# A stick-breaking and RWKV-7 block with 32 experts: weights in transfers of 512 KB, experts in an order that alternates the groups, scatters counted by buffer

## The reference

```python
group_logits = (hf @ w_rg)                       # 4 groups
group_idx = jnp.argmax(group_logits, axis=-1)
group_gate = take(softmax(group_logits), group_idx)
exp_logits = (hf @ w_re).reshape(n_tok, 4, 8)    # 8 experts a group
in_group = take(exp_logits, group_idx)
top_p, top_i = lax.top_k(softmax(in_group), 2)
gates = group_gate * top_p / sum(top_p)
eid = group_idx * 8 + top_i                      # two experts a token, one group
y[token] = sum over the two of gate * ((silu(x @ w_g[e]) * (x @ w_u[e])) @ w_d[e])
x = x + y
```

## Time and profile before

| | us |
|---|---|
| median of 3 runs | 3158.65 (3153.46 to 3159.69) |
| the profiled execution | 3158.47 |
| its span | 3156.7 |
| TensorE busy in the span | 2846.0 (90%) |
| GpSimd busy in the span | 856.1 (27%) |
| granted TensorE clock, mean | 0.961 |

### The profile page before, as it was taken

The page is one execution under the profiler, slowest core; times in us unless marked ns, Lnnn a source line. Parts: engine busy times, 40 slices in busy tenths (PEclk is TensorE's granted clock), DMA queues, the critical chain, the costliest instruction groups (busy, mean ns, idle before and its releaser), DMA issues. The chain is left out here.

```text
span 3156.7 us, 86816 instructions
## 1 busy us (share of the span) xinstructions
PE 2846.0 (90%) x36552; PEld 1661.1 (53%) x36553; DVE 1225.1 (39%) x2272; ACT 974.8 (31%) x2057; POOL 856.1 (27%) x1110
## 2 busy tenths in 40 slices
PE   8999999999999996888888899678899888888888
PEld 4444444445666665777776455444444444444444
DVE  2323221115888775776764344511111111111111
ACT  1111100004666664555543343311111111111111
POOL 0000300001011006666653000133344334334334
PEclk9999999999999998999999999789989999999999
DMA  3212221112102201111110554156766766666663
GB/s 124 67 50 66 79 88 60 56 45 91 54 19 64 90 9 31 44 42 41 38 52 12 182 200 159 47 189 217 242 200 216 249 201 213 218 225 196 226 212 72
DMA packets 187461, 369.99 MB, mean 117 GB/s; under 512 B 30449, under 2 KB 130289, under 8 KB 168178
## 3 DMA queue, kind: packets, MB, share of 16 engines
q1 hardware_dynamic: 159458, 328.71, 28.9%
q0 software_dynamic: 27792, 38.16, 6.7%
HBM read 296.30 MB, written 70.52 MB: 116 GB/s over the span
## 5 line engine op out<-in xcount | busy, mean ns | idle before, releaser
L2260 PE MATMUL gu_ps<-wg_,xT 128*32 128x256 f32 x3136 | 386.0, 389 | 8.1 <-issue 5.7
L2228 POOL DMA_INDIRECT out<-y,put x144 | 230.6, 1601 | 590.8 <-issue 426.7
L2260 PE MATMUL gu_ps<-wu_,xT 128*32 128x256 f32 x3136 | 385.9, 389 | 0.0
L712 DVE TENSOR_TENSOR_SCAN h_all<-h_all 128x512 f32<-128x512 f32 (+3 forms) x320 | 345.8, 1129 | 69.0 <-ACT h_all L664 42.9
L344 PE MATMUL ps<-low,high 128*128 128x512 f32 x768 | 337.9, 597 | 2.4 <-issue 2.4
L2275 PE MATMUL y_ps<-wd_,hT 128*32 128x256 f32 x4608 | 322.6, 427 | 0.0
L2356 DVE COPY xT<-xT_ps 128x128 f32<-128x128 f32 x145 | 42.3, 292 | 660.9 <-PE xT_ps L2254 660.9
L2260 PEld LDWEIGHTS gu_ps<-wg_,xT 128*32 128x32 f32 x3136 | 181.3, 113 | 146.5 <-issue 34.2
L1707 PE MATMUL ps<-high 128*128 128x512 f32 x512 | 230.9, 601 | 8.7 <-DMA high<-mixT 8.3
L344 PEld LDWEIGHTS ps<-low,high 128*128 128x128 f32 x768 | 144.6, 192 | 173.6 <-issue 173.6
L690 POOL TENSOR_SCALAR_AFFINE_SELECT h_all<-h_all 128x256 f32<-128x256 f32 x64 | 39.7, 620 | 703.6 <-ACT h_all L664 703.4
(11 more groups left out here) (321 smaller groups left out, 4586.9 us busy)
## 6 DMA issues: line engine op xcount, KB each, us to landing
wd_<-in_w_exp_down SPq DMA_DIRECT2D x32, 2048.0 KB
wg_<-in_w_exp_gate SPq DMA_DIRECT2D x22, 2048.0 KB
wu_<-in_w_exp_up SPq DMA_DIRECT2D x22, 2048.0 KB
high<-in_w_exp_gate SPq DMA_DIRECT2D x10, 2048.0 KB
high<-in_w_exp_up SPq DMA_DIRECT2D x10, 2048.0 KB
pT<-low SPq DMA_DIRECT2D x13, 1024.0 KB, 3.9
rkv<-pT SPq DMA_DIRECT2D x96, 128.0 KB, 2.5
high<-in_x SPq DMA_DIRECT2D x16, 512.0 KB, 4.0
```

The costliest lines, as they stand in the source:

```text
L712: dve.tensor_tensor_scan(prod[:, n % KEPT, h, 0:w][:, ::-1], rows, rows, so_far, ALU.mult, ALU.bypass).then_inc(scanned, 1)
L2228: pool.indirect_dma_start(out=out_quarters[:, :], out_offset=bass.IndirectOffsetOnAxis(ap=put[j][:, 0:1], axis=0), in_=y[j][:, :], in_offs ...
L2260: last = pe.matmul(gu_ps[QUARTERS[q], 0:256], xT[:, k % 2, k // 2, :], w[s][:, k, half * 256:(half + 1) * 256], start=(k == 0), stop=(k == ...
```

## The change

Four things, in one diff:

1. `load` issues each 2 MB matrix as four transfers of 512 KB. For gate and up a partition's row of 8 KB in a transfer becomes two rows of 4 KB in two transfers; for down it has been rows of 4 KB before.
2. The experts are numbered `place in the group * 4 + group` and not `group * 8 + place in the group`, so that neighbours in the order are of different groups and share no token. `load` turns the turn into the expert.
3. Scatters count on two semaphores, one for each buffer of y. ACT and DVE wait for their buffer's last scatter, GpSimd for none.
4. Blocks alternate between two sets of spare rows, so that two scatters don't add to the same spare row. The output tensor is 32 rows longer.

```diff
@@ ExpertWeights
-    def load(self, sp, e, s, part=None):
+    def load(self, sp, turn, s, part=None):
         w_g, w_u, w_d = self.dram
+        e = turn % N_GROUPS * PER_GROUP + turn // N_GROUPS
         for x, (to, src) in enumerate(((self.wg, w_g), (self.wu, w_u))):
             if part in (None, x):
-                sp.dma_start(to[s][:, :, :].rearrange("p (h k) f -> p h (k f)", h=2),
-                             src[0, bass.ds(e, 1), :, :].rearrange("o (h p k) f -> p (o h) (k f)", h=2, p=P)).then_inc(self.gu_loaded[s], 16)
+                rows = src[0, bass.ds(e, 1), :, :].rearrange("o (h p k) f -> p (o h) k f", h=2, p=P)
+                for h in range(2):
+                    for ks in (slice(0, 2), slice(2, 4)):
+                        sp.dma_start(to[s][:, 4 * h + ks.start:4 * h + ks.stop, :], rows[:, h, ks, :]).then_inc(self.gu_loaded[s], 16)
         if part in (None, 2):
-            sp.dma_start(self.wd[s][:, :, :], w_d[0, bass.ds(e, 1), :, :].rearrange("o (f p) d -> p (o f) d", p=P)).then_inc(self.d_loaded[s], 16)
+            rows = w_d[0, bass.ds(e, 1), :, :].rearrange("o (f p) d -> p (o f) d", p=P)
+            for f in range(FF // P):
+                sp.dma_start(self.wd[s][:, f, :], rows[:, f, :]).then_inc(self.d_loaded[s], 16)
@@ mix_out_and_route
-                    dve.tensor_scalar(gidx_8[:, :], gidx[:, :], float(PER_GROUP), None, ALU.mult)
...
-                    dve.tensor_scalar(eid[:, :], eidx[:, :], gidx_8[:, :], None, ALU.add)
+                    dve.tensor_scalar(eid[:, :], eidx[:, :], float(N_GROUPS), gidx[:, :], ALU.mult, ALU.add)
@@ place_slots
-        spare_i, spare = sb("spare_i", [P, 1], I32), sb("spare", [P, 1])
+        spare_i, spare = sb("spare_i", [ROWS, TABLE], I32), sb("spare", [ROWS, TABLE])
...
-                pool.iota(spare_i[:, :], pattern=[[0, 1]], base=SEQ + 1, channel_multiplier=1)
+                pool.iota(spare_i[:, :].rearrange("p (b j) -> p b j", j=2), pattern=[[0, TABLE // 2], [ROWS, 2]], base=SEQ + 1, channel_multiplier=1)
...
-                dve.tensor_scalar(empty[:, :], token_ps[LO, 0:TABLE], 0.0, spare[LO, :], ALU.is_equal, ALU.mult)
+                dve.scalar_tensor_tensor(empty[:, :], token_ps[LO, 0:TABLE], 0.0, spare[:, :], ALU.is_equal, ALU.mult)
@@ run_experts, gpsimd
                     pool.drain()
-                    stores_done(pool, b)
-                    pool.sem_inc(on_pool, 1)
                     pool.wait_ge(y_copied, b * 2 + CREDIT + 2)
                     pool.sem_inc(on_pool, 1)
                     pool.indirect_dma_start(out=out_quarters[:, :], out_offset=bass.IndirectOffsetOnAxis(ap=put[j][:, 0:1], axis=0),
-                                            in_=y[j][:, :], in_offset=None, compute_op=ALU.add).then_inc(stored, 16)
+                                            in_=y[j][:, :], in_offset=None, compute_op=ALU.add).then_inc(stored[j], 16)
@@ run_experts, scalar; vector has the same
-                def copy_y(b, j):
+                def copy_y(b, j, i):
                     act.wait_ge(y_done, b + 1)
-                    stores_done(act, b - 1)
+                    if not isinstance(i, int) or i > 0:
+                        act.wait_ge(stored[j], i * 16)
                     act.copy(y[j][LO, :], y_ps[LO, 0:256]).then_inc(y_copied, 1)
@@ run_experts, tensor
-                    pe.wait_ge(gu_loaded[s], n * 32 + 32)
-                    pe.wait_ge(d_loaded[s], n * 16 + 16)
+                    pe.wait_ge(gu_loaded[s], n * 128 + 128)
+                    pe.wait_ge(d_loaded[s], n * 64 + 64)
```

More of the change, by code:

```diff
@@ L1741, in mix_out_and_route @@
         gidx8, eidx8 = sb("gidx8", [P, 8], U32), sb("eidx8", [P, 8], U32)
-        negmax, gidx, gidx_8, gsum, ggate = [sb(n, [P, 1]) for n in ("negmax", "gidx", "gidx_8", "gsum", "ggate")]
+        negmax, gidx, gsum, ggate = [sb(n, [P, 1]) for n in ("negmax", "gidx", "gsum", "ggate")]
         gexp = sb("gexp", [P, N_GROUPS])
@@ L2155, in run_experts @@
         names = """consts gathered turned xT_ready gu_done silu_ready h_ready h_turned hT_ready
-            y_done y_copied stored""".split()
+            y_done y_copied""".split()
         (consts, gathered, turned, xT_ready, gu_done, silu_ready, h_ready, h_turned, hT_ready,
-         y_done, y_copied, stored) = [sem(f"p7_{n}") for n in names]
+         y_done, y_copied) = [sem(f"p7_{n}") for n in names]
+        stored = [sem(f"p7_stored{j}") for j in range(2)]
         on_pe, on_pool = program.gates_passed
@@ L2170, in pairs_of, with last_pair @@
             return eng.value_load(n_pairs[0:1, 0:1], min_val=NE, max_val=MAX_BLOCKS // 2)
-        def last_block(eng):
-            return eng.value_load(n_pairs[0:1, 1:2], min_val=NE - 1, max_val=MAX_BLOCKS // 2 - 1) * 2 + 1
+        def last_pair(eng):
+            return eng.value_load(n_pairs[0:1, 1:2], min_val=NE - 1, max_val=MAX_BLOCKS // 2 - 1)
         def pairs_of_blocks(eng, pairs, one_block):
             for b in range(4):
-                one_block(b, b % 2, first=(b == 0))
+                one_block(b, b % 2, b // 2, first=(b == 0))
             with eng.Fori(2, pairs) as i:
                 for j in range(2):
-                    one_block(i * 2 + j, j, first=False)
-        def stores_done(eng, blocks):
-            if not isinstance(blocks, int) or blocks > 0:
-                eng.wait_ge(stored, blocks * 16)
+                    one_block(i * 2 + j, j, i, first=False)
         give_credit(nc, y_copied)
@@ L2215, in next_rows, with one_block @@
                     pool.tensor_copy(take[j][:, :], from_all[:, bass.ds(b, 1)])
-                def one_block(b, j, first):
+                def one_block(b, j, i, first):
                     pool.wait_ge(turned, b + 3)
@@ L2243, in _ @@
                 pool.sem_inc(on_pool, 1)
-                pool.wait_ge(stored, pairs * 32)
-                pool.sem_inc(on_pool, 1)
+                for j in range(2):
+                    pool.wait_ge(stored[j], pairs * 16)
+                    pool.sem_inc(on_pool, 1)
                 pool.drain()
@@ L2342, in one_block @@
                     if not first:
-                        copy_y(b - 1, 1 - j)
+                        copy_y(b - 1, 1 - j, i - 1 + j)
                     act.wait_ge(h_turned, b + 1)
@@ L2349, in _ @@
                 pairs_of_blocks(act, pairs_of(act), one_block)
-                copy_y(last_block(act), 1)
+                last = last_pair(act)
+                copy_y(last * 2 + 1, 1, last)
             @block.vector
@@ L2356, in copy_xT, with copy_y, one_block @@
                     dve.tensor_copy(xT[:, 1, :, :], xT_ps[1][:, 0:P].rearrange("p (q t) -> p q t", q=4)).then_inc(xT_ready, 1)
-                def copy_y(b, j):
+                def copy_y(b, j, i):
                     dve.wait_ge(y_done, b + 1)
-                    stores_done(dve, b - 1)
+                    if not isinstance(i, int) or i > 0:
+                        dve.wait_ge(stored[j], i * 16)
                     dve.tensor_copy(y[j][HI, :], y_ps[HI, 0:256]).then_inc(y_copied, 1)
-                def one_block(b, j, first):
+                def one_block(b, j, i, first):
                     dve.tensor_copy(gate[j][HI, :], gate_all[HI, bass.ds(b, 1)])
@@ L2370, in one_block @@
                     if not first:
-                        copy_y(b - 1, 1 - j)
+                        copy_y(b - 1, 1 - j, i - 1 + j)
                 copy_xT(0)
                 pairs_of_blocks(dve, pairs_of(dve), one_block)
-                copy_y(last_block(dve), 1)
+                last = last_pair(dve)
+                copy_y(last * 2 + 1, 1, last)
 def hybrid_block(nc, x, norm1_gain, w_in, sb_q_gain, sb_k_gain, rw_shift_mu, rw_w0, rw_w_up, rw_a0, rw_a_up, rw_g_up,
@@ L2432 @@
         aps.append(nc.dram_tensor(f"in_{name}", a.shape, mybir.dt.from_np(a.dtype), kind="ExternalInput").ap())
-    out = nc.dram_tensor("out", (1, SEQ + ROWS, D), F32, kind="ExternalOutput").ap()
+    out = nc.dram_tensor("out", (1, SEQ + 2 * ROWS, D), F32, kind="ExternalOutput").ap()
     hybrid_block(nc, *aps, out)
```

## The result

The changed kernel takes 3171.14 us (median of 20 runs, 3157.32 to 3181.29), the kernel before 3158.35 us in the same comparison (20 runs, 3150.11 to 3172.39). The ratio is 1.004, with a 95% interval of 1.0028 to 1.0051: slower by 13 us, where I had forecast 45 us faster. The profiled execution took 3167.7 us, with a span of 3166.0.

The account below looks back on a forecast made before the run. Gathers landing late under weight loads, and the slow clock after, were taken to cost 6.6 us a load; 0.9 + 2.5 + 1.7 = 5.1 instead, over 29 loads, with small terms gains 45 us: 3113 us, range 3035 to 3172.

Parts of the forecast that it names:

- What bounds the kernel: In `run_experts`, late gathers and the slow clock after idle time lose 190 us over 29 refills, 6.6 us each.
- the landing L: Time until a gather lands in the thick of a load: 5.6 us taken, bounds 4.0 and 7.1.
- The 4.0 us row: Profiled gather issued at 2425.14, landing after 4.0 us with only the tail of 4 KB rows left; L's lower bound.
- L - 4.71: TensorE's idle time in a load's first block, 1.25 + L + 0.13 - 6.09: 0.9 us forecast, 3.25 before.
- the base: Loss per refill in the kernel before, from the whole `run_experts` stage: 6.6 us.
- Second gather: Second loaded block: GpSimd arrives 2.5 us earlier and meets more load, giving back part; idle L - 3.12 = 2.5 us.
- Weights in 512 KB: SP's weight loads: 12 issues instead of 3 still fill the DMA engines for about the same 18 us.
- rival 3: Small transfers run at three quarters of the rate, a third gather falls into the load: 78 us more, 3236 us; 3%.
- Two scatters under way: On GpSimd the drain still keeps scatters apart; only sequencer steps go, 0.16 us, shortening 3.13 to 2.97 in loaded pairs.
- Order of the experts, SP's issues: Alternating groups change neither blocks nor refills: zero; extra weight issues ahead of routing's row loads: zero, bounds 0 and 9 us.
- Rival 2: Gather delay comes from a fixed backlog of bytes, L near 6.6, then 5.5: 32 us more, 3190 us; 15%.
- Rival 4: If the drain let the next scatter go before the gather lands, idle is L - 4.71 per block: 3020 us; inside 28%.

Follow-up runs that it names:

- experiment 5: Changed kernel without GpSimd's drain, with 2 MB transfers: 3072.57 us; that with gathers one block further ahead: 3066.13; drainless with paced loads: 3007.20 (512 KB), 2986.14 (2 MB).
- experiment 1: Kernel before with only 512 KB transfers: 3176.48 us; changed kernel with 2 MB transfers: 3142.67 us; kernel before with only the change's stores: 3146.03 us.

## Why the prediction was wrong

- **What bounds the kernel.** Right in size: 6.6 us a refill, 6.4 measured by leaving loads out. The sum treated a late second gather and a slow clock as terms that add. In the changed kernel the second block takes 9.07 us from turn to turn (2395.01 to 2404.08), which is 6.1 + 2.97, the gather's chain. TensorE at the clock of 0.72 fills most of it, and only 1.3 us are idle. The slow clock and the late gather lie beside each other there, and the longer of the two counts.
- **The failed step: the landing L.** I reasoned "half as long packets mean half the delay", took 5.6 us for both gathers of a load, and had 4.0 as a lower bound. Measured: 7.4 us in the median for the first, up to 8.4, and 6.1 for the second. With rows of 8, 4 and 2 KB the first is 7.9, 6.9 to 7.4 and 7.0. What a load adds before the first packet of a scatter or gather, some 2.5 us, is the same for all three (experiment 5). The 4.0 us row showed the end of a load, not short rows; the prediction said "the tail" and used it all the same. With L = 8.1, my own formula L - 4.71 gives the 3.4 us that were measured. With 7.4 and 6.1 the prediction's own terms are 2.7 + 3.0 + 1.7 = 7.4 us a load, 0.8 above the base: some 23 us slower instead of 45 faster. So the mis-sized L alone turns the sign of the sum.
- **Second gather.** That it would give something back was right, for the wrong reason. The first lands only 0.5 us sooner, so GpSimd is hardly early; the load lasts 2.3 us longer, and the second gather takes 6.1 us for 4.0. In the load shown that is hidden beside the slow clock: 3.4 + 3.0 = 6.4 us against 3.2 + 3.0 before. Over the stage the small transfers cost the 12 to 28 us of experiment 1.
- **Weights in 512 KB.** "About the same 18 us" was wrong for 4 KB rows of gate and up: 20.0 us for 17.7, with 279 against 362 GB/s at the start of a load. The `w_out` train that I took for the rate moves other data. The Trainium skill's advice of at least 1 MiB a batch ("DMA: Bandwidth & Descriptors", section Bandwidth) stood as rival 3. The runs don't bear it out as a matter of size: 1 MB transfers with 4 KB rows are no faster than 512 KB, and 1 MB with 8 KB rows no slower than 2 MB.
- **Two scatters under way.** Right: the drain keeps them apart, since in the changed kernel a scatter's last packet comes at least 1.7 us before the next scatter's issue, and 2.97 us was met. Beside 2 MB transfers its worth is 14 us where I had 5, and the clock is higher there, 0.95 for 0.93; beside the small ones of the changed kernel it is the 5 or less.
- **Order of the experts, SP's issues.** Nothing that these runs could tell, as said.
- **Rivals.** Rival 2 (a fixed backlog of bytes) was nearest in cause and had the sign. It asked for a first L near 6.6 and a second of 5.5, and gave 3190; measured are 7.4 and 6.1. That the time still is 3171 I put down to the overlap of clock and wait; this is argued and not shown. The stores aren't the reason, since the small transfers alone take 3176. I held it at 15% because "gathers that met 4 KB rows did land sooner", which was the tail again. Rival 4's remark on a kernel in which the drain lets the scatter go was right in form (idle L - 4.71 in each block: 6.53 gives 1.8, and 1.7 was measured), but with L of 6.5 and 5.6 the time without the drain is 3065 us and not 3020.

The time of 3171 us lies at the very edge of my range, and the sign was wrong.

## What to carry to other kernels

When an edit removes a wait, look at the wait or drain that stands ahead of it on the same engine: if that ends later, the edit frees almost nothing, and the one ahead is the thing to remove. A delay read at the end of a burst of traffic says nothing about its middle; bound a newcomer's delay by rows from the thick of the load, look at what stands ahead of it on its own queue, and don't scale it with the packet's length unless a row shows that it does. Where small latency-bound transfers share the DMA engines with bulk loads, issue the bulk piece by piece, each just behind a small one, so that little of it is queued when the next small one comes.

## What the runs showed of the hardware

- GpSimd's drain ends 0.12 us after the landing of an indirect DMA issued ahead of it (median over the loop's blocks), and costs to some 0.2% what an explicit wait for that landing costs (ratios 1.0040 and 1.0019).
- The first gather behind a 6 MB load lands after 6.9 to 7.9 us in the median, with weight rows of 8, 4 or 2 KB and transfers of 2 MB to 256 KB; in a quiet block it is 2.8.
- A scatter issued as a load begins sends its first packet after 4.8, 4.9 to 5.1 and 4.8 us (medians) beside weight rows of 8, 4 and 2 KB, in a quiet block after 2.2. A gather in a load whose scatter has passed 2 us earlier still takes 4.2 us to its first packet, in a quiet block 1.7.
- Rows of 4 KB that take half of each 8 KB stretch of the weights move 279 to 321 GB/s in the first six microseconds of a load (medians) where 8 KB rows move 362 to 370. The load lasts 19.7 to 20.0 us instead of 17.5 to 17.7. Later in the load both reach 380 to 403.
- With 16 to 35 us of idle time of TensorE in the stage the mean granted clock is 1.00, with 88 us 0.99, with 127 to 148 us 0.93 to 0.95.
